# The input and weights of the per-layer projection move from the expert ring's extra slots to other tiles

## The chip, the cores and the metric

The kernel runs on one core of a Trainium2 chip. The metric is the device time in microseconds (us) of one execution; the time of a kernel is the median of its runs. All data are float32.

## What is computed

A two-layer decoder step for 256 prompt tokens and 8 decode tokens (264 columns, `T`), width 1024 (`D`). Layer 0 mixes with a Mamba-2 block, layer 1 with native sparse attention. Each layer ends in the same tail, which is where the change lies:

```python
def moe(h, router_w, router_bias, w_gate, w_up, w_down):
    score = sigmoid(h @ router_w)                  # 16 experts in 4 groups
    # the best group by score + bias, the two best experts in it, gates normed to 1
    out = 0
    for e in range(16):
        hid = silu(h @ w_gate[e]) * (h @ w_up[e])  # 1024 -> 512
        out = out + gate[..., e:e + 1] * (hid @ w_down[e])
    return out

def layer_tail(x, mix, p_i, ...):
    h = layer_norm(ALPHA * x + mix)
    h = layer_norm(ALPHA * h + moe(h, ...))
    return h + sigmoid(h @ ple_gate) * (p_i @ ple_proj)
```

`p_i @ ple_proj` is the per-layer projection: 256 to 1024, eight output tiles of 128 by 264.

## The kernel before

**Layout and staging.** Activations are kept with features on the 128 partitions and tokens along the free axis: `xT`, `acc` and `ple` are tiles of [128, 8, 264]. The program has four blocks one after the other: the Mamba block, `tail(0)`, the attention block, `tail(1)`. In each block every engine has an instruction stream of its own, and semaphores order them. All waits are written by hand.

**Expert weights.** An expert's gate, up and down matrices are each one unit of 2 MiB, [128, 4096]. Experts are taken in pairs, so a pair has six units: `n = 6 i + r`, where r = 0, 1 is gate, 2, 3 is up and 4, 5 is down. Units 48 and 49 are the two halves of `ple_gate`. Unit n lies in slot `n % 8`. Slots 0 to 5 are in `expert_ring`, which lives through the whole program; slots 6 and 7 are the tile `expert_ring_more` (`ring2`), which exists only in the tail. Slots 0 to 5 are loaded ahead of the tail or at its start (in the second tail units 3 to 5 are issued in the tail itself). All unit loads are issued by SP, in order of n. From unit 8 on SP waits until the slot is free: units 8 and 9 and 10 and 11 wait for the gate and the up half of pair 0 (`gu_done`), units 12 and 13 for its down half (`down_done`), and so on for later pairs (L979 to L985 of the program).

**The projection.** Its input `pT` (264 KB) and its weights `wple` (1 MB) lie in slot 6, that is in `ring2[:, 0]`. So SP's unit loads 6 and 7 stand behind a wait for the last projection: `sp.wait_ge(e_proj, KD * (L + 1))`. TensorE runs `project(0)` and `project(1)` before the router's rank matmuls and `project(2)` to `project(7)` after the first slot matmul (L1031). Tile m goes to one of two PSUM banks, and ScalarE copies it to `ple[:, m, :]` (L1197); `project(m)` waits for the copy of tile m - 2. `ple` is read only at the end of the tail (L1381).

**The start of pair 0.** ScalarE writes the token rows to HBM (L1194), POOL gathers the rows of a pair's 128 slots back (L1252) once these writes have landed and the slot numbers are there, TensorE transposes them (`turn_rows`, L1082), ScalarE packs them into `xg` (`pack`, L1204), and `gate_up(0)` begins (L1097). `pack(0)` stands behind all eight copies of `ple` in ScalarE's stream. After `gate_up(0)` come `other_slots` (L1057), `turn(0)` (L1106) and `down(0)` (L1119), then `gate_up(1)`. For pairs 1 and on, `scatter(i - 1)` (L1130) stands between `gate_up(i)` and `turn(i)`.

Of the kernel before, what the change touches and what calls it, by code (L numbers as in the profile page):

```python
# [20 lines left out]
P = 128  # L21
D = 1024
KD = D // P
SEQ = 256
DB = 8
T = SEQ + DB
# [13 lines left out]
NE, FF, EG = 16, 512, 4  # L40
# [18 lines left out]
def trunk(nc, I, O):  # L59
    root = ExitStack()  # L60
    with root:
# [842 lines left out]
        def tail(L, out=None):  # L904

            ld_p, e_done, e_sig, e_out, e_proj, e_pre = ple_sems
# [5 lines left out]
            with ExitStack() as st:  # L912
# [3 lines left out]
                ple = sb("ple_projected", [P, KD, T])  # L916
                acc = sb("acc", [P, KD, T])
                ring2 = sb("expert_ring_more", [P, 2, CH])
# [5 lines left out]
                xg = sb("x_packed", [P, KD, 2 * CAP])  # L924
                sg = sb("silu_gate", [P, FF])
                hid = sb("hid", [P, FF])
                ht = sb("hid_T", [P, NF, 2 * CAP])
# [5 lines left out]
                sel1 = sb("slot_onehot", [P, 3, NE * CAP])  # L933
                idxf, idxi, gcol = sb("slot_token", [P, NP2]), sb("slot_token_int", [P, NP2], I32), sb("slot_gate", [P, NP2])

                pT = ring2[:, 0, 0:2 * T].rearrange("p (k t) -> p k t", k=2)
                wple = ring2[:, 0, 2 * T:2 * T + 2 * D].rearrange("p (k n) -> p k n", k=2)
                scT = sg[0:NE, 0:T]
                xtok = [xrow[:, 0, :], xrow[:, 1, :], ys[:]]
                over = xrow[:].rearrange("p a b -> p (a b)")  # L940
# [5 lines left out]
                ob = [st.enter_context(nc.psum_tensor(f"mo{L}{n}", [P, 512], F32)) for n in range(4)]  # L946
# [19 lines left out]
                with nc.Block() as block:  # L966
                    @block.sync
                    def _(sp):
                        sp.dma_start(pT, I["pT"][L].rearrange("(k p) t -> p k t", p=P)).then_inc(ld_p, 16)
                        sp.dma_start(wple, I["ple_proj"][L].rearrange("p (k n) -> p k n", k=2)).then_inc(ld_p, 16)  # L970
                        if L == 1:
                            for n in range(3, 6):
                                load_unit(sp, L, n, unit(n))
                        sp.wait_ge(e_proj, KD * (L + 1))
                        for n in range(6, 8):
                            load_unit(sp, L, n, unit(n))
                        for n in range(8, 6 * NP2 + 2):
                            i, r = (n - 8) // 6, (n - 8) % 6
                            if r < 4:  # L979
                                sp.wait_ge(gu_done, n2 + 2 * i + 1 + r // 2)  # L980
                            else:
                                sp.wait_ge(down_done, n1 + i + 1)
                            load_unit(sp, L, n, unit(n))

                        def over_load(e):  # L985
                            sp.wait_ge(o_dve, NDV * e + 1)
                            for w, name in enumerate(("moe_w_gate", "moe_w_up", "moe_w_down")):
                                src = I[name][bass.ds(NE * L + e, 1)].rearrange("a p n -> (a p) n")
                                sp.dma_start(ring[:, 1, w * CH:(w + 1) * CH], src).then_inc(o_ld, 16)
                        sp.wait_ge(r_over, L + 1)  # L990
                        sp.wait_ge(gu_done, n2 + 2 * NP2)
                        sp.wait_ge(down_done, n1 + NP2)
                        overflow(sp, over_load)
                        if L == 0:
                            page = [page_number(sp, n) for n in range(2 * NPG)]
                            load_cmp(sp, 0, page)
                            sp.wait_ge(ln_sems[0], 2 * L + 2)
                            for c in range(2):
                                load_chunk(sp, c, I["nsa_w_in"][c])
                            sp.wait_ge(e_done, 4)  # L1000
                            load_cmp(sp, 1, page)
                        if out is not None:
                            for m in range(0, KD, 2):
                                sp.wait_ge(e_out, KD * L + m + 2)
                                store(sp, out[:, m:m + 2, :], xT[:, m:m + 2, :])

                    @block.tensor
                    def _(pe):
                        tr, mm = nc.tensor.transpose, nc.tensor.matmul
                        ln_a.pe(pe)  # L1010

                        for k in range(KD):
                            ln_a.out_ready(pe, k)
                            last = mm(hb[0][0:NE, 0:T], rw[:, k, :], xT[:, k, :], start=k == 0, stop=k == KD - 1)  # L1014
# [9 lines left out]

                        def project(m):
                            if m == 0:
                                pe.wait_ge(ld_p, 32 * L + 32)
                            if m >= 2:
                                pe.wait_ge(e_pre, KD * L + m - 1)
                            for k in range(2):  # L1030
                                last = mm(ob[2 + m % 2][:, 0:T], wple[:, k, m * P:(m + 1) * P], pT[:, k, :], start=k == 0, stop=k == 1)  # L1031
                            last.then_inc(e_proj, 1)

                        turn_x(0)
# [2 lines left out]
                        for q, (t0, n) in enumerate(tile3):  # L1037
                            last = tr(hb[1][0:n, q * NE:(q + 1) * NE], scT[:, t0:t0 + n], ident[0:NE, 0:NE])
# [144 lines left out]
                    def _(act):  # L1183
# [9 lines left out]
                                act.wait_ge(r_xtok, 6 * L + c + 1)  # L1193
                                act.dma_start(x_rows[L][t0:t0 + n, :], xtok[c // 2][0:n, :]).then_inc(r_rows, 16)  # L1194
                        for m in range(KD):
                            act.wait_ge(e_proj, KD * L + m + 1)
                            A_(ple[:, m, :], ob[2 + m % 2][:, 0:T], ACT.Copy).then_inc(e_pre, 1)  # L1197

                        def pack(i):
# [960 lines left out]
```

## Time and profile before

| | us |
|---|---|
| median of 3 runs | 1167.97 |
| lowest and highest run | 1164.39, 1169.42 |
| the profiled execution, device time | 1171.1 |
| its span, first to last instruction | 1169.3 |
| TensorE busy | 1051.3 (90%) |
| VectorE busy | 469.3 (40%) |
| ScalarE busy | 297.0 (25%) |
| DMA over the span | 347.36 MB, mean 297 GB/s |

The first tail lies at about 300 to 600 us of the span, the second at 843 to 1169. PE is TensorE's matmuls, PEld its weight loads (beside them), DVE is VectorE, ACT ScalarE, POOL GpSimd; SPq, ACTq and POOLq are the instructions with which these engines issue DMAs. PEclk is the share of TensorE's full clock that was granted: 1.0 is 2.4 GHz, 0.5 is 1.2 GHz, and a mean between them is a stretch that had some of both. Brackets behind an instruction give the idle time of its engine ahead of it and what ended it. Matmuls are pipelined, so a busy PE isn't PE at its peak.

### The profile page before, as it was taken

The page shows a single profiled execution, that of the slowest core. Times are in us where ns is not written, and L with a number is a line of the kernel's source. Part 1 is how long each engine was busy: PE and PEld are TensorE (multiplying, and loading weights), DVE is VectorE, ACT ScalarE, POOL GpSimd, SP SyncE. Part 2 cuts the span into 40 slices and gives each one's busy share as a digit, 9 for nine tenths or more (in the row PEclk, how much of TensorE's full clock was granted, in tenths as well). Part 3 has the DMA queues.
Part 4 walks back from the last instruction along what each step waited for, and adds up shares of the span by engine and source line. Part 5 has one row for each costly group of instructions (what it writes and reads, how often), then busy time and mean ns, then how long its engine had stood idle before and what let it go on. Part 6 is the DMA issues. An engine that isn't in the chain of part 4 may idle for free. (4 is left out here: it accounts for less than half of the span.)

```text
span 1169.3 us, 14744 instructions
## 1 busy us (share of the span) xinstructions
PE 1051.3 (90%) x5243; PEld 658.4 (56%) x5243; DVE 469.3 (40%) x1383; ACT 297.0 (25%) x765; POOL 133.3 (11%) x121
## 2 busy tenths in 40 slices
PE   7899998698799999899799989779989999989868
PEld 5688775587554444344477875345755344444347
DVE  2769898932331112011355977472161111111132
ACT  2211798700321111111220015362051011101031
POOL 0000013300001000000004724452000000000000
PEclk9899998799988999999999998889988999999989
DMA  8744696675959999999556975949368899999901
GB/s 287 248 163 149 220 278 215 198 281 198 399 225 408 427 429 428 425 427 428 213 216 235 339 262 178 370 136 382 128 265 370 363 427 426 428 428 426 417 4 38
DMA packets 88943, 347.36 MB, mean 297 GB/s; under 512 B 14690, under 2 KB 52578, under 8 KB 72322
## 3 DMA queue, kind: packets, MB, share of 16 engines
q1 hardware_dynamic: 81186, 313.57, 69.3%
q10 hardware_dynamic: 5376, 24.40, 5.3%
q0 software_dynamic: 2304, 8.39, 1.8%
q8 instruction: 45, 0.74, 0.3%
q14 instruction: 32, 0.26, 0.1%
HBM read 331.66 MB, written 23.04 MB: 303 GB/s over the span
## 5 line engine op out<-in xcount | busy, mean ns | idle before, releaser
L1097 PE MATMUL mh<-expert_ring,x_packed 128*64 128x512 f32 x768 | 173.0, 606 | 14.6 <-DMA expert_ring<-in_moe_w_up 12.7
L1349 DVE TENSOR_TENSOR hid<-mh,silu_gate 128x512 f32<-128x512 f32 x16 | 11.1, 692 | 374.8 <-PE mh L1097 325.9
L1097 PEld LDWEIGHTS mh<-expert_ring,x_packed 128*64 128x64 f32 x768 | 58.2, 140 | 126.3 <-issue 124.3
L1119 PE MATMUL mo<-expert_ring,hid_T 128*64 128x512 f32 x384 | 89.1, 618 | 1.4 <-ACT hid_T L1218 1.4
L495 PE MATMUL ss<-xT,expert_ring 128*128 128x264 f32 x384 | 90.0, 395 | 0.0
L1563 PE MATMUL na<-xT,expert_ring 128*128 128x264 f32 (+1 forms) x336 | 78.8, 398 | 6.1 <-DMA expert_ring<-in_nsa_w_in 3.3
L495 PEld LDWEIGHTS ss<-xT,expert_ring 128*128 128x128 f32 x384 | 73.8, 195 | 13.8 <-issue 0.8
L1563 PEld LDWEIGHTS na<-xT,expert_ring 128*128 128x128 f32 (+1 forms) x336 | 64.6, 193 | 20.2 <-DMA expert_ring<-in_nsa_w_in 4.1
L506 PE MATMUL ss<-xT,expert_ring 128*128 128x264 f32 x256 | 64.1, 406 | 6.1 <-ACT z L385 6.1
L1179 PE MATMUL mg<-acc,expert_ring 128*128 128x264 f32 x256 | 61.7, 406 | 7.2 <-ACT acc L883 7.2
L1097 PE MATMUL mh<-expert_ring_more,x_packed 128*64 128x512 f32 x256 | 58.3, 609 | 7.7 <-DMA expert_ring_more<-in_moe_w_up 3.6
L1252 POOL DMA_INDIRECT x_rows_packed<-x_rows,slot_token_int x16 | 15.6, 973 | 430.6 <-DVE slot_token_int L1312 219.2
L609 PE MATMUL ss<-conv_out,expert_ring 128*128 128x264 f32 x256 | 59.2, 394 | 4.9 <-DVE conv_out L838 4.2
L1179 PEld LDWEIGHTS mg<-acc,expert_ring 128*128 128x128 f32 x256 | 51.4, 202 | 17.5 <-issue 8.0
L506 PEld LDWEIGHTS ss<-xT,expert_ring 128*128 128x128 f32 x256 | 49.3, 198 | 19.5 <-ACT z L385 9.3
L1119 PEld LDWEIGHTS mo<-expert_ring,hid_T 128*64 128x64 f32 x384 | 27.4, 142 | 55.0 <-issue 51.2
L609 PEld LDWEIGHTS ss<-conv_out,expert_ring 128*128 128x128 f32 x256 | 49.7, 195 | 14.2 <-DVE conv_out L838 4.6
L1218 ACT ACTIVATE hid_T<-mo 128x512 f32<-128x512 f32 x16 | 9.6, 599 | 171.8 <-PE mo L1106 171.8
L1097 PEld LDWEIGHTS mh<-expert_ring_more,x_packed 128*64 128x64 f32 x256 | 20.1, 140 | 44.3 <-issue 41.9
L1227 ACT ACTIVATE y_slots<-mo 128x512 f32<-128x512 f32 x32 | 17.4, 595 | 108.8 <-PE mo L1119 108.8
L1130 PE MATMUL mo<-scatter_gates,y_slots 128*128 128x264 f32 x128 | 40.6, 399 | 2.4 <-ACT y_slots L1227 2.4
L126 POOL TENSOR_TENSOR expert_ring<-expert_ring,pos_softmax 128x1024 f32<-128x1024 f32 x14 | 39.4, 2839 | 20.6 <-DMA expert_ring<-in_cmp_pages 20.6
(377 smaller groups left out, 1541.1 us busy)
## 6 DMA issues: line engine op xcount, KB each, us to landing
expert_ring<-in_moe_w_down SPq DMA_DIRECT2D x24, 2048.0 KB, 22.3
expert_ring<-in_moe_w_gate SPq DMA_DIRECT2D x24, 2048.0 KB, 17.2
expert_ring<-in_moe_w_up SPq DMA_DIRECT2D x24, 2048.0 KB, 23.5
expert_ring<-in_ssd_w_in SPq DMA_DIRECT2D x10, 2048.0 KB, 7.9
expert_ring_more<-in_moe_w_gate SPq DMA_DIRECT2D x8, 2048.0 KB, 14.7
expert_ring_more<-in_moe_w_up SPq DMA_DIRECT2D x8, 2048.0 KB, 19.2
expert_ring_more<-in_moe_w_down SPq DMA_DIRECT2D x8, 2048.0 KB, 22.5
expert_ring<-in_cmp_pages SPq DMA_DIRECT2D x40, 256.0 KB, 4.5
```

Source lines behind the costliest of these rows:

```text
L126: return eng.tensor_tensor(x, x, wb[:, a:a + 1, :].unsqueeze(1).to_broadcast([P, NPG, 2, BLK]), ALU.mult)
L495: last = mm(pt[m % 4][:, 0:T], wc[:, k, ((m - 1) % 4) * P:((m - 1) % 4 + 1) * P], xT[:, k, :], start=k == 0, stop=k == KD - 1)
L506: last = mm(z_bank[:, 0:T], wc[:, k, (j % 4) * P:(j % 4 + 1) * P], xT[:, k, :], start=k == 0, stop=k == KD - 1)
L609: last = mm(o_bank[m][:, 0:T], w_at[k // 2][:, (k % 2) * D + m * P:(k % 2) * D + (m + 1) * P], cv[:, k, :], start=k == 0, stop=k == JX - 1)
L1097: last = mm(hb[w][s * CAP:(s + 1) * CAP, :], xg[:, k, s * CAP:(s + 1) * CAP], unit(6 * i + 2 * w + s)[:, k * FF:(k + 1) * FF], start=k == ...
L1119: last = mm(ob[2 + a][s * CAP:(s + 1) * CAP, :], ht[:, k, s * CAP:(s + 1) * CAP], unit(6 * i + 4 + s)[:, o:o + 512], start=k == 0, stop=k ...
L1130: mm(sc_bank[d % 4][:, 0:T], ys[:, d * P:(d + 1) * P], sgt[:, i, :], start=True, stop=True).then_inc(sc_done, 1)
L1179: last = mm(gb[m % 2][:, 0:T], wc[:, k, (m % 4) * P:(m % 4 + 1) * P], acc[:, k, :], start=k == 0, stop=k == KD - 1)
L1227: A_(ys[:, a * 512:(a + 1) * 512], ob[2 + a][:], ACT.Copy).then_inc(ys_ok, 1)
L1252: nc.gpsimd.indirect_dma_start(xrow[:, i % 2, :], None, x_rows[L][:, :], bass.IndirectOffsetOnAxis(idxi[:, i:i + 1], 0)).then_inc(row[i % ...
L1349: V.tensor_tensor(hid[:], hb[1][:], sg[:], ALU.mult).then_inc(hid_ok, 1)
L1563: last = mm(pb[m % 8][0:M, 0:T], wc[:, k, (m % 4) * P:(m % 4) * P + M], xT[:, k, :], start=k == 0, stop=k == KD - 1)
```

## The change

`pT` moves to the last two tiles of `ple` itself. The weights are split in three: the second half (k = 1) goes to `xg`, and the first half (k = 0) to `hid` and to `ht`. All three are tiles that pair 0 of the mixture writes for the first time after the projections. They are loaded by three DMAs in the place of one, so the load count that `project(0)` waits for goes from 32 to 64 per layer. SP no longer waits for `e_proj` ahead of units 6 and 7. ScalarE's copy of tile 6 writes where `pT` lies, and so waits for all eight projections; the copies of the other tiles wait as before.

```diff
--- before.py
+++ after.py
@@ -933,8 +933,9 @@
                 sel1 = sb("slot_onehot", [P, 3, NE * CAP])
                 idxf, idxi, gcol = sb("slot_token", [P, NP2]), sb("slot_token_int", [P, NP2], I32), sb("slot_gate", [P, NP2])
 
-                pT = ring2[:, 0, 0:2 * T].rearrange("p (k t) -> p k t", k=2)
-                wple = ring2[:, 0, 2 * T:2 * T + 2 * D].rearrange("p (k n) -> p k n", k=2)
+                pT = ple[:, 6:8, :]
+                wple1 = xg[:].rearrange("p k c -> p (k c)")
+                wple = lambda k, m: wple1[:, m * P:(m + 1) * P] if k else (hid, ht[:].rearrange("p f c -> p (f c)"))[m // 4][:, (m % 4) * P:(m % 4 + 1) * P]
                 scT = sg[0:NE, 0:T]
                 xtok = [xrow[:, 0, :], xrow[:, 1, :], ys[:]]
                 over = xrow[:].rearrange("p a b -> p (a b)")
@@ -967,11 +968,12 @@
                     @block.sync
                     def _(sp):
                         sp.dma_start(pT, I["pT"][L].rearrange("(k p) t -> p k t", p=P)).then_inc(ld_p, 16)
-                        sp.dma_start(wple, I["ple_proj"][L].rearrange("p (k n) -> p k n", k=2)).then_inc(ld_p, 16)
+                        sp.dma_start(wple1, I["ple_proj"][L][:, D:2 * D]).then_inc(ld_p, 16)
+                        sp.dma_start(hid[:], I["ple_proj"][L][:, 0:FF]).then_inc(ld_p, 16)
+                        sp.dma_start(ht[:].rearrange("p f c -> p (f c)"), I["ple_proj"][L][:, FF:D]).then_inc(ld_p, 16)
                         if L == 1:
                             for n in range(3, 6):
                                 load_unit(sp, L, n, unit(n))
-                        sp.wait_ge(e_proj, KD * (L + 1))
                         for n in range(6, 8):
                             load_unit(sp, L, n, unit(n))
                         for n in range(8, 6 * NP2 + 2):
@@ -1024,11 +1026,11 @@
 
                         def project(m):
                             if m == 0:
-                                pe.wait_ge(ld_p, 32 * L + 32)
+                                pe.wait_ge(ld_p, 64 * L + 64)
                             if m >= 2:
                                 pe.wait_ge(e_pre, KD * L + m - 1)
                             for k in range(2):
-                                last = mm(ob[2 + m % 2][:, 0:T], wple[:, k, m * P:(m + 1) * P], pT[:, k, :], start=k == 0, stop=k == 1)
+                                last = mm(ob[2 + m % 2][:, 0:T], wple(k, m), pT[:, k, :], start=k == 0, stop=k == 1)
                             last.then_inc(e_proj, 1)
 
                         turn_x(0)
@@ -1193,7 +1195,7 @@
                                 act.wait_ge(r_xtok, 6 * L + c + 1)
                                 act.dma_start(x_rows[L][t0:t0 + n, :], xtok[c // 2][0:n, :]).then_inc(r_rows, 16)
                         for m in range(KD):
-                            act.wait_ge(e_proj, KD * L + m + 1)
+                            act.wait_ge(e_proj, KD * L + min(m + 1 + m // 6, KD))
                             A_(ple[:, m, :], ob[2 + m % 2][:, 0:T], ACT.Copy).then_inc(e_pre, 1)
 
                         def pack(i):
```

## Rows read from the trace of the kernel before

**Rows 1.** The page's busy share of the DMA engines in tenths, 40 equal slices of 29.2 us.

```profile
DMA  8744696675959999999556975949368899999901
```

**Rows 2.** Chain that ended last, second tail: start us, us, what, count.

```profile
969.68 13.73 PE mh L1097 x64
...
995.50 6.89 PE mh L1097 x32
...
1062.00 30.46 DMA expert_ring<-in_moe_w_up
...
1092.60 8.45 PE mh L1097 x32
```

**Rows 3.** Timeline of SP: start us, us to issue, line, tiles, count.

```profile
300.89 0.47 SPq L970 DMA_DIRECT2D expert_ring_more<-in_ple_proj  x1
...
337.12 0.80 SPq L110 DMA_DIRECT2D expert_ring_more<-in_moe_w_gate  x2
...
345.83 0.80 SPq L110 DMA_DIRECT2D expert_ring<-in_moe_w_up  x2
...
370.32 1.00 SPq L110 DMA_DIRECT2D expert_ring<-in_moe_w_gate  x2
...
879.53 0.81 SPq L110 DMA_DIRECT2D expert_ring_more<-in_moe_w_gate  x2
...
915.70 0.81 SPq L110 DMA_DIRECT2D expert_ring<-in_moe_w_gate  x2
```

**Rows 4.** Stretches: us, busy us (count) by engine, PEclk, DMA share, GB/s.

```profile
324.00:325.00 1.00, 0.69 (x6) 0.70 (x6) 0.83 (x6) 0.29 (x2) 0.00 (x0) 1.00 0.25 33
...
370.00:371.00 1.00, 0.75 (x6) 0.48 (x5) 0.00 (x0) 0.68 (x2) 0.00 (x0) 1.00 0.77 311
...
914.00:915.00 1.00, 1.00 (x6) 0.28 (x4) 0.00 (x0) 0.00 (x0) 0.00 (x0) 1.00 0.04 16
...
325.00:330.00 5.00, 3.95 (x23) 3.46 (x23) 2.45 (x16) 0.00 (x0) 0.59 (x1) 0.74 0.00 0
...
338.00:370.00 32.00, 30.61 (x145) 14.02 (x145) 3.87 (x13) 3.51 (x6) 2.00 (x2) 0.89 1.00 415
...
881.00:914.00 33.00, 32.21 (x139) 16.11 (x141) 3.87 (x13) 2.92 (x5) 1.99 (x2) 0.79 0.96 405
```

**Rows 5.** Timeline of the first tail, TensorE and ScalarE: start us, us, engine, line.

```profile
321.57 1.95 PE L1031 MATMUL mo<-expert_ring_more 128*128 128x264 f32 x8
...
323.62 0.67 ACT L1197 ACTIVATE ple_projected<-mo 128x264 f32<-128x264 f32 x2 [0.38 <-PE mo L1031]
...
324.31 0.39 PE L1050 MATMUL mh<-insel,m 128*128 128x16 f32 x2 [0.79 <-DVE insel L1291]
...
328.86 8.23 PE L1031 MATMUL mo<-expert_ring_more 128*128 128x264 f32 x24
...
337.13 0.39 ACT L1197 ACTIVATE ple_projected<-mo 128x264 f32<-128x264 f32 x1 [0.50 <-PE mo L1031]
...
337.56 1.08 ACT L1204 ACTIVATE x_packed<-mg 128x512 f32<-128x512 f32 x2
...
338.70 13.95 PE L1097 MATMUL mh<-expert_ring,x_packed 128*64 128x512 f32 x64 [0.74 <-ACT x_packed L1204]
...
547.21 7.09 PE L1097 MATMUL mh<-expert_ring,x_packed 128*64 128x512 f32 x32 [1.62 <-DMA expert_ring<-in_moe_w_up]
```

**Rows 6.** DMAs issued about 300.9, 329.4 and 360.9: engine, count, KB, us to landing.

```profile
expert_ring_more<-in_ple_proj SPq DMA_DIRECT2D x1, 1024.0 KB, 20.2
...
x_rows_packed<-x_rows,slot_token_int POOLq DMA_INDIRECT x1, 4.5
...
x_rows_packed<-x_rows,slot_token_int POOLq DMA_INDIRECT x1, 11.7
```

**Rows 7.** Timeline: second write of token rows, and the first gather.

```profile
321.80 0.33 ACTq L1194 DMA_DIRECT2D x_rows<-x_rows_packed  x1
...
329.41 1.12 POOL L1252 DMA_INDIRECT x_rows_packed<-x_rows,slot_token_int  x1 [90.10 <-DVE slot_token_int L1312]
```

## The prediction, made before the changed kernel was run

> **What bounds the kernel now.** Read the DMA line of the page first [rows 1]: there are two long plateaus of nines, slices 13 to 19 and 33 to 38. These are the two mixtures of experts (one per tail), each of which streams 48 expert units and two gate units of 2 MiB. The chain of waits then says who holds the end [rows 2]. In the second mixture it runs on TensorE through pairs 0 to 3, and later it passes through transfers of moe_w_up that land 30 us after issue. From there the order is set by bytes, not by matmuls. So a tail has two halves. A front half is paced by TensorE (router, projection, pair 0). A back half is paced by the DMA engines, and the question is which instant starts the back half's clock.
>
> The timeline of SP [rows 3] answers. Units 6 and 7, which the change moves, go out at 337.12 and 879.53, when the last of the eight projections has ended. Units 8 to 11 follow when gate_up(0) frees slots. The next pair, 12 and 13, can't go before down(0) has read slots 4 and 5: 370.32 and 915.70. That is an instant of TensorE's front half. The DMA engines are idle ahead of 337.12 (no bytes at all from 325 to 330) [rows 4], which is the hole the change fills. But they are also just running empty when 12 and 13 are issued. At 370 to 371 the share is 0.77, and in the second tail they are at 16 GB/s from 914 to 915 [rows 4].
>
> The two tails are a natural experiment on whether a head start there is kept. In the first, units 8 to 11 were barely finished at 370.32; in the second there was a hole of some 2 us before 915.70. From the issue of 12 and 13 to the start of the up half of pair 7, the last one that waits for a load, the first tail takes 547.21 - 370.32 = 176.89 us [rows 3, 5] and the second 1092.60 - 915.70 = 176.90 us [rows 2, 3]. A hole ahead of that issue costs nothing. The back half starts when down(0) ends, and what was loaded before doesn't enter.
>
> **The change part by part.**
>
> *Units 6 and 7 go out behind the projection's loads* (about 302 and 845) and not at 337.12 and 879.53. They land some 12 us later, in the hole. Their first reader is gate_up(1), which starts behind down(0) and turn_rows(1). In either tail it doesn't wait for units 6 and 7 now, since they were issued 33 and 36 us earlier. Gain there: 0. Units 8 to 11 keep their issue times (gate_up(0) sets them); they find an empty queue and land earlier. Their readers are the down half of pair 0, which reads 4 and 5 and not these, and pair 1, which doesn't wait either. Gain: 0. Units 12 and 13 keep their issue time; in the second tail the queue was empty already, so 0. In the first tail an old remainder was still in the queue: at most the 1 us of the row at 370 [rows 4], and by the equal 176.9 us nothing. I take 0, with -1 to 0 as bounds. The hole isn't removed, it is moved to just before 370.
>
> *The copies of ple.* The input p now lies in columns 6 and 7 of ple, so ScalarE may write tile 6 only after all eight projections and not after the seventh. Tile 7 is unchanged in its wait but now stands behind tile 6. Today the copy of tile 7 starts at 337.13, pack(0) at 337.56, and gate_up(0) at 338.70, with nothing between them [rows 5]. After: tile 6 starts at 337.13, tile 7 behind it. Two copies back to back take 0.67 us where one takes 0.39 [rows 5], so the second costs 0.28; with a whole copy as the other bound, 0.28 to 0.39 us, straight on the path gather, pack, gate_up(0), down(0), issue of 12. In the second tail the same order holds. Sum: +0.6 to +0.8, I take +0.7. The projections themselves are not slowed: project(7) needs copies 0 to 5 only.
>
> *Two loads more per tail.* ple_proj comes in three pieces and not in one; the bytes are the same. SP spends 0.47 us on the one issue now [rows 3], so two more put everything behind them about 0.9 us later. In the first tail the projection's weights land at 300.89 + 20.2 = 321.1 [rows 3, 6] behind five units, and project(0) starts at 321.57 [rows 5]. Because the queue is full at that time, the landing follows the bytes and not the issue: 0. If it moved by the whole 0.9, project(0) would start 0.4 late, and TensorE has 0.79 us of waiting for VectorE right behind project(1) [rows 5] that takes it up. Cost 0; without that cover at most 0.4. In the second tail the loads find a short queue 20 us ahead of their use: 0. Units 3, 4 and 5 of the second tail go out 0.9 us later, which nobody notices: they are read from 888 on.
>
> *The token rows beside units 6 and 7.* This is what the change newly exposes. ScalarE writes the token rows to HBM (512 KiB issued at 321.80, as much 1.5 us before) and POOL gathers them back at 329.41 [rows 7]. The gather takes 4.5 us alone and 11.7 us beside unit loads [rows 6], so sharing costs up to 7 us per transfer. Today both have the engines to themselves: the writes are through by 325 [rows 4]. The gather is in at 333.9 and is needed when the projections end, 328.86 + 8.23 = 337.1 [rows 5]; slack 3.2 us. After the change 4.19 MB of loads and 1.05 MB of writes share the engines from 321.1. At 415 GB/s [rows 4] they are all through after 12.6 us, at 333.7, whatever the order. In the worst case the gather goes only then and lands at 338.2, that is 1.1 us late. In the best case the writes get half, finish by about 327, and the gather waits for nothing new. The second tail has nearly the same distances. Bounds 0 to +1.5 in each tail, 0 to +3 together. I take 0, because the writes are a quarter of the load's bytes, and a share of a half would clear them in 5 us.
>
> The Trainium skill ("DMA: Bandwidth & Descriptors", section on queues, rings and completion order) says that each engine goes round-robin between the queues with work, packet by packet, and that a completion mark lands only behind all earlier writes of that engine across its queues. The first half favours the small write, and the sum with it would be my 0. The second half would hold the write's completion behind load data written before it, and with it the sum would go towards the +3. The 11.7 us against 4.5 agrees with sharing, and does not say which half decides.
>
> **The sum**, against the profiled execution's own 1171.1 us (span 1169.3 and 1.8 around it): +0.7, no gain, gives 1171.8. That execution lies 3.1 us above the median of 1168.0, so the forecast for the median is 1168.0 + 0.7 = **1168.7 us**.
>
> **A disturbance of the same size.** From the issue of 6 to that of 12, the same instructions take 370.32 - 337.12 = 33.2 us in the first tail and 36.2 us in the second [rows 3]. The granted clock is 0.89 and 0.79 in these stretches [rows 4], a matter of how long it stayed at 1.2 GHz. So each tail can be off by 3 us either way, for no reason in the program. The three times before lie between 1164.4 and 1169.4.
>
> **Rivals.**
> - *The head start is kept.* If the back half's clock were running from units 6 and 7 on, taking 4.19 MB at 415 GB/s off it would save 10.1 us in each tail: 1168.7 - 20.2 = 1148.5 us. For it: both mixtures end bound by loads [rows 2]. Against: the queue runs empty before 12 and 13, and the equal 176.9 us. Chance 0.06.
> - *Token rows late, and the clock with them* (the slower side). It acts at the gather of pair 0, and decides once that lands later than 337.1. It costs up to 3 us as above. TensorE then stands idle just ahead of gate_up(0), coming out of a stretch at 1.2 GHz. If gate_up(0) (13.95 us for 64 matmuls [rows 5]) ran its first half at that clock, it would lose 7 us a tail; half of that is the likelier size. Together 0.7 + 3 + 7 = 10.7: 1178.7 us. For it: 11.7 against 4.5 us. Against: at most 1.5 us of idle time a tail, and idle gaps as long stand in that stretch already. Chance 0.07.
> - *The late rows without the clock*: up to 1171.7 us. Chance 0.10, inside the same band.
> - *The change doesn't load earlier*, since the units wait in the full queue of the first tail anyway: they go 20 us earlier all the same once it drains at 321. If not, only the 0.7 stays: 1168.7 us. Chance 0.02.
>
> **How the numbers follow.** Forecast 0.75, late rows 0.10, no earlier load 0.02, the two far cases 0.06 and 0.07. About 0.5% (5.8 us) is what a measurement of this kernel can tell from no change. Within it lie forecast, late rows and no earlier load, 0.87, less 0.04 for both tails' clock falling on one side: 0.83. Faster 0.08 (0.06 + 0.02), slower 0.09 (0.07 + 0.02). For the range I go 3 us of clock and 1 of the first tail's remainder below 1168.7, 1164.5, and 3 of clock and half of the late rows above, 1173.2. It leaves out both far cases.
>
> **What would show it.** Right: DMA bytes from 321 to 333 where there were none, an idle hole of 3 us or more before units 12 and 13 in both tails, and again 176.9 us from their issue to pair 7's up half; pack(0) 0.3 us later after the last projection. Wrong: an issue of 12 more than 1 us nearer to or farther from the last projection at equal clock, gate_up(0) waiting for the gathered rows, or project(0) waiting for its weights by more than 0.8 us. The forecast falls if 176.9 us becomes clearly less.

## The result and the profile after

The changed kernel takes 1189.67 us where the kernel before takes 1168.70; the ratio is 1.018 with an interval of 1.014 to 1.022. That is slower by about 21 us, outside the range of 1164.5 to 1173.2. One of the changed kernel's four runs took 1608.9 us at a granted clock of 0.625 and is left out of the ratio. The profiled execution took 1189.74 us with a span of 1188.0, 18.7 us more than the span before.

The DMA line of the page (40 slices, now of 29.7 us):

```profile
DMA  9753786766938999999555975949394899999900
```

The two plateaus are as long as before to within a slice [rows 1]. What changed lies ahead of them. The timeline of SP, for both tails:

```profile
302.40 4.00 SPq L110 DMA_DIRECT2D expert_ring_more<-in_moe_w_gate  x2
...
352.10 0.80 SPq L110 DMA_DIRECT2D expert_ring<-in_moe_w_up  x2
...
379.62 0.80 SPq L110 DMA_DIRECT2D expert_ring<-in_moe_w_gate  x2
...
859.30 1.11 SPq L110 DMA_DIRECT2D expert_ring_more<-in_moe_w_gate  x2
...
935.89 0.80 SPq L110 DMA_DIRECT2D expert_ring<-in_moe_w_gate  x2
```

Units 6 and 7 do go out 35 us earlier in the first tail (302.40, 337.12 before [rows 3]). But the next pair goes out at 352.10 and not 345.83, and units 12 and 13 at 379.62 and not 370.32. The first tail's start, taken as the issue of `pT`, is the same, 300.45 and 300.46. The timeline of the first tail says why:

```profile
335.36 1.11 POOL L1254 DMA_INDIRECT x_rows_packed<-x_rows,slot_token_int  x1 [96.07 <-DMA x_rows<-y_slots]
...
337.12 0.67 ACT L1199 ACTIVATE ple_projected<-mo 128x264 f32<-128x264 f32 x2 [1.39 <-PE mo L1033]
...
340.23 1.20 PE L1084 MATMUL mg<-ident,x_rows_packed 128*128 128x128 f32 x8 [3.15 <-DMA x_rows_packed<-x_rows,slot_token_int]
...
342.12 16.81 PE L1099 MATMUL mh<-expert_ring,x_packed 128*64 128x512 f32 x64 [0.69 <-ACT x_packed L1206]
...
358.86 8.62 PE L1059 MATMUL mo<-token_and_gates,slot_onehot 128*128 128x17 f32 x42
```

POOL's first gather stands at 335.36 (329.41 before [rows 7]), and its releaser is the last of ScalarE's three writes of token rows, issued 12.1 us earlier, at 323.25. TensorE waits 3.15 us for the gathered rows behind the projections. The matmuls of gate_up(0) then take 16.81 us where they took 13.95 [rows 5]. The stretches of 1 us and more (columns as in [rows 4]) show both halves, the DMA engines ahead of the gather and the clock behind it:

```profile
332.00:333.00 1.00, 1.00 (x4) 0.76 (x3) 1.00 (x2) 0.29 (x1) 0.00 (x0) 0.50 0.45 180
...
333.00:334.00 1.00, 1.00 (x4) 0.79 (x3) 0.76 (x1) 0.10 (x1) 0.00 (x0) 0.50 0.11 45
...
338.00:341.00 3.00, 0.77 (x7) 0.77 (x8) 0.00 (x0) 0.08 (x1) 0.00 (x0) 1.00 0.33 128
...
342.00:348.00 6.00, 5.88 (x14) 1.71 (x16) 0.00 (x0) 1.35 (x2) 0.00 (x0) 0.51 0.00 0
...
349.00:360.00 11.00, 11.00 (x57) 4.07 (x53) 0.69 (x1) 0.60 (x1) 0.00 (x0) 1.00 0.64 253
```

The loads and writes end between 333 and 334. There is no traffic of units from then to 353. The granted clock is 1.00 while TensorE waits, 0.51 at 342 to 348, behind the gap, and back at 1.00 from 348. The chain of waits runs through the same place in the second tail, where the writes take 12.44 us to land:

```profile
877.53 12.44 DMA x_rows<-y_slots
...
890.74 4.83 DMA x_rows_packed<-x_rows,slot_token_int
...
895.62 1.98 PE mg L1084 x8
...
898.27 16.92 PE mh L1099 x64
```

Cutting both spans at the same marks gives the whole of the 18.7 us. "Start" is the issue of `pT`; "up half" is the start of the up half of pair 7.

| stretch | before | after | difference |
|---|---|---|---|
| first tail, start to issue of units 12, 13 | 69.86 | 79.17 | +9.3 |
| from there to the up half | 176.89 | 177.04 | +0.2 |
| up half to the start of the second tail | 295.60 | 299.15 | +3.5 |
| second tail, start to issue of 12, 13 | 72.89 | 80.08 | +7.2 |
| from there to the up half | 176.90 | 177.25 | +0.3 |
| up half to the end | 76.70 | 74.86 | -1.8 |

The two front halves carry 16.5 us. In them gate_up(0) starts 3.4 and 4.2 us later against the tail's start, 7.6 together; 0.9 of the 4.2 is the transposes and the packing ahead of it, with eight transposes in 1.98 us where they took 1.04. The other 8.9 us is the same instructions taking longer: gate_up(0) +2.9 and +3.0, the slot matmuls +2.1 and -0.3, down(0) +1.0 and +0.3 (with their gaps, 5.9 and 3.0). The start isn't a steady mark to the microsecond: the first write of token rows follows it by 19.8 us in both first tails, and by 19.9 us before and 18.8 after in the second. The middle row isn't touched by the change. It is between 292.8 and 306.1 us in the profiles of the kernels below, without an order that follows their edits, so its +3.5 is taken as scatter.

### The profile page after: what moved, and what is told of

Read it like the earlier page. It is cut to its first block and busy times, and to the rows that moved or that the text cites. A ratio compares the mean times of both kernels' runs of the same rounds, so it can differ in the third digit from the quotient of the medians.

```text
span 1188.0 us, 14748 instructions
## 1 busy us (share of the span) xinstructions
PE 1060.8 (89%) x5243; PEld 660.6 (56%) x5243; DVE 468.7 (39%) x1383; ACT 296.3 (25%) x765; POOL 133.1 (11%) x121
## 5 line engine op out<-in xcount | busy, mean ns | idle before, releaser
L1099 PE MATMUL mh<-expert_ring,x_packed 128*64 128x512 f32 x768 | 180.7, 627 | 16.5 <-DMA expert_ring<-in_moe_w_up 14.2
L1565 PE MATMUL na<-xT,expert_ring 128*128 128x264 f32 (+1 forms) x336 | 75.7, 387 | 7.1 <-DMA expert_ring<-in_nsa_w_in 4.3
L506 PE MATMUL ss<-xT,expert_ring 128*128 128x264 f32 x256 | 64.2, 406 | 6.0 <-ACT z L385 6.0
L126 POOL TENSOR_TENSOR expert_ring<-expert_ring,pos_softmax 128x1024 f32<-128x1024 f32 x14 | 39.3, 2833 | 19.9 <-DMA expert_ring<-in_cmp_pages 19.9
```

The source lines that it names most:

```text
L126: return eng.tensor_tensor(x, x, wb[:, a:a + 1, :].unsqueeze(1).to_broadcast([P, NPG, 2, BLK]), ALU.mult)
L506: last = mm(z_bank[:, 0:T], wc[:, k, (j % 4) * P:(j % 4 + 1) * P], xT[:, k, :], start=k == 0, stop=k == KD - 1)
L1099: last = mm(hb[w][s * CAP:(s + 1) * CAP, :], xg[:, k, s * CAP:(s + 1) * CAP], unit(6 * i + 2 * w + s)[:, k * FF:(k + 1) * FF], start=k == ...
L1565: last = mm(pb[m % 8][0:M, 0:T], wc[:, k, (m % 4) * P:(m % 4) * P + M], xT[:, k, :], start=k == 0, stop=k == KD - 1)
```

## The experiments

Theory A: the early loads keep the DMA engines busy, the writes of token rows land late, the gather with them, and TensorE's clock falls behind the gap. Rivals: the new tiles and the pieces of the load cost by themselves (B); the head start has a worth that something hides (C). The times below stand beside the median of the kernel before in the same measurement, 1167 to 1169 us. The ratio in brackets is an estimate of its own with its interval, and differs by up to 0.2% from the quotient of the two medians.

**Only the tiles are new.**

```diff
+                        sp.wait_ge(e_proj, KD * (L + 1))
                         for n in range(6, 8):
                             load_unit(sp, L, n, unit(n))
```

> The changed kernel with the wait for the last projection put back ahead of units 6 and 7: input and weights lie in the new tiles and come in four loads, but units 6 and 7 go out when they did before. Theory A (the early loads take the DMA engines from the token rows, so the first gather lands late, and TensorE falls to 1.2 GHz behind the gap): all of the 20 us goes, only the copy order stays, 0.3 us a tail: about 1168.5 us, within 3 us of the kernel before; the writes of token rows are through 3 us after the last is issued, the gather goes at 329.4 and lands at 333.9. Rival B (the new tiles, the pieces of ple_proj or the order of the copies cost): stays at 1185 to 1190.

Measured: 1169.06 us, ratio 1.0003 (0.9983 to 1.0023). Rival B is out. The tiles, the three pieces of `ple_proj` and the order of the copies together cost nothing that the times can show; the whole loss comes from issuing units 6 and 7 early.

**Units 6 and 7 behind the writes, and behind the gather.** The line put in is `sp.wait_ge(r_rows, 48 * (L + 1))` in the first and `sp.wait_ge(r_row0, 16 * (4 * L + 1))` in the second.

> The changed kernel, with SP waiting for the token rows' writes (not for the projections) ahead of units 6 and 7. They go out at about 326 and run beside the first gather. Theory A in its form A1 (what shares the engines with unit loads drains with them, to the end of the loads' bytes): loads through at about 338.5, gather in at 338 to 340, gate_up(0) 1 to 3 us late and the clock low behind it, 1174 to 1182 us. Form A2 (a short transfer gets about half of the engines): gather in by 335, nothing late, 1168 to 1170 us. Rival B: 1185 to 1190 us. Rival C (the head start is worth something once the rows aren't late): below 1164 us.

> The changed kernel, with SP waiting for the first gather's landing ahead of units 6 and 7: they go out at about 334, 3 us ahead of the last projection's end, and share the engines with nothing the front half needs. Theory A, with the back half counted from the end of down(0): as the kernel before, 1167 to 1170 us, and again 176.9 to 177.3 us from the issue of units 12 and 13 to pair 7's up half. Rival C (the head start is worth what it is long): 3 us a tail less, 1162 us. Rival B: 1185 to 1190 us.

Measured: 1181.42 us behind the writes (1.0122, 1.0083 to 1.0161), 1167.81 us behind the gather (1.0008, 0.9979 to 1.0037). In the first, units 6 and 7 go out at 324.64, and the gather at 327.58. Its issue and landing, and TensorE's wait:

```profile
x_rows_packed<-x_rows,slot_token_int POOLq DMA_INDIRECT x1, 11.0
...
338.60 1.97 PE L1085 MATMUL mg<-ident,x_rows_packed 128*128 128x128 f32 x8 [4.27 <-DMA x_rows_packed<-x_rows,slot_token_int]
...
341.25 16.02 PE L1100 MATMUL mh<-expert_ring,x_packed 128*64 128x512 f32 x64 [0.69 <-ACT x_packed L1207]
```

The gather takes 11.0 us where it takes 4.5 alone [rows 6], and the wait of 4.27 us has 16 us of gate_up(0) behind it. Protecting the writes is not enough; the gather needs the engines as well. With both protected the loss is gone:

```profile
332.60 0.80 SPq L110 DMA_DIRECT2D expert_ring_more<-in_moe_w_gate  x2
...
332.71 1.04 PE L1085 MATMUL mg<-ident,x_rows_packed 128*128 128x128 f32 x8
```

The time is that of the kernel before. But units 6 and 7 go out only 0.1 us ahead of the transposes behind the last projection (1.6 us in the second tail, 877.45 and 879.05). So short a head start doesn't test rival C; e11_acc_later does, below.

**The gap filled.**

```diff
+                        for j in range((7, 10)[L]):
+                            mm(hb[1][:, 0:T], ones[:], xT[:, 0, :], start=True, stop=True)
                         turn_rows(0)
```

> The changed kernel with 7 (first tail) and 10 (second tail) matmuls of 128x264 added on TensorE in the place where it waits for the first gather; their result is overwritten and not used. If the loss beyond the late gather is the clock's (theory A): gate_up(0) runs at 2.4 GHz in 14 us and not in 16.8, the gather is as late as in the changed kernel; the first tail gets back 3 to 6 us and the second 3 us, 1180 to 1184 us. If the clock is set by the small slot matmuls behind gate_up(0) and not by the gap: gate_up(0) in 14 us, but 8.6 us for the slot matmuls as before, 1184 to 1186 us. If the gap has nothing to do with the clock: 1189 us or more.

Measured: 1180.54 us (1.0124, 1.0081 to 1.0168), 9 us less than the changed kernel by the medians and 6 by the ratios, with more work in it. The two intervals overlap, so the times alone don't carry it; the trace does.

```profile
342.07 13.95 PE L1099 MATMUL mh<-expert_ring,x_packed 128*64 128x512 f32 x64 [0.74 <-ACT x_packed L1208]
...
355.96 8.84 PE L1059 MATMUL mo<-token_and_gates,slot_onehot 128*128 128x17 f32 x42
...
342.00:348.00 6.00, 5.93 (x28) 2.06 (x30) 0.00 (x0) 1.30 (x2) 0.00 (x0) 1.00 0.01 3
```

gate_up(0) starts when it did in the changed kernel (342.07, 342.12), but at a clock of 1.00 and in 13.95 us. The slot matmuls behind it are slow here as well (8.84 us in this tail, 7.00 in the second), so their clock doesn't hang on the gap. The front halves of the table are 76.04 and 75.98 us here, 3.1 and 4.1 us shorter than in the changed kernel, with gate_up(0) starting within 0.3 us of where it did there. So 7.2 of the table's 8.9 us come back, and 5.9 of them are gate_up(0) (13.95 us in both tails). Why the slot matmuls are slow stays open.

**Half of the bytes, and more of them.** In the first kernel only unit 6 is early. In the second everything is as in the changed kernel, and two copies of 2 MiB from HBM to HBM are queued behind unit 7.

> The changed kernel with only unit 6 early; unit 7 waits for the last projection as before. Half the bytes share the engines with the token rows: 2.1 MB of load and 1.05 MB of writes are through 7.6 us after the projection's weights, at about 329, and land by 330.5. If the rows land when the bytes queued beside them are through (theory A1): the gather goes at 330 to 331 and lands by 335.5, ahead of the projections' end, so no loss in either tail: 1167 to 1171 us. If rows beside any load take their 12 us (A3, a fixed delay): the gather goes at 335.4 and the loss is the whole one, 1186 to 1190 us. Rival B': 1185 to 1190 us from the number of loads.

> The changed kernel with 4.2 MB more of copies (HBM to HBM, into a buffer nobody reads) queued on SP behind units 6 and 7 in each tail, so that the queue beside the token rows stays full for some 10 us longer. Units 12 and 13 wait for them in TensorE's stream, where they are long done. If rows drain with what is queued beside them (A1): the writes land near 343 to 348, the gather goes then and lands 5 us later, gate_up(0) starts 8 us or more later than in the changed kernel, 1205 us or more. If a row write beside a full queue takes its 12 us whatever is queued (A3): the writes land at 335.4 as in the changed kernel, and only the gather is slower, 11 to 12 us where it was 4.8: gate_up(0) at 349 where it was 342.1.

Measured: 1175.36 us (1.0074, 1.0044 to 1.0105) and 1211.6 us (one run). The first gather of each, with what released it, and the wait of TensorE in the second:

```profile
330.64 2.85 POOL L1256 DMA_INDIRECT x_rows_packed<-x_rows,slot_token_int  x1 [90.92 <-DMA x_rows<-y_slots]
```

```profile
345.73 1.11 POOL L1260 DMA_INDIRECT x_rows_packed<-x_rows,slot_token_int  x1 [107.19 <-DMA x_rows<-y_slots]
...
350.61 1.97 PE L1088 MATMUL mg<-ident,x_rows_packed 128*128 128x128 f32 x8 [14.58 <-DMA x_rows_packed<-x_rows,slot_token_int]
...
342.00:343.00 1.00, 0.00 (x0) 0.00 (x0) 0.00 (x0) 0.00 (x0) 0.00 (x0) 0.50 0.24 98
...
343.00:344.00 1.00, 0.00 (x0) 0.00 (x0) 0.00 (x0) 0.00 (x0) 0.00 (x0) 0.50 0.01 0
```

The landing of the rows releases POOL at 330.6, 335.4 or 345.7, for 2.1, 4.2 or 8.4 MB queued beside them (in the last, 4.2 of loads and 4.2 of copies). Each time it is 1.6 to 2.7 us after the DMA engines go quiet (329, 333.5 and 343). So form A1 holds for the writes, and the fixed 12 us is out: that number came from the size of the queue. Unit 6 alone, though, should have cost nothing by this sum, and it costs 7 us. TensorE waits 2.47 and 2.68 us for the gather there, and gate_up(0) takes 15.57 and 16.00 us. That had another cause.

**The scaling of acc.** In the kernel with one early unit POOL's gather instruction takes 2.85 us, where it takes 1.12 [rows 7]. VectorE's timeline beside it:

```profile
328.33 3.01 DVE L1311 TENSOR_TENSOR slot_onehot<-slot,slot_numbers 128x1792 f32<-128x1792 f32 x2
...
331.26 1.24 DVE L1336 TENSOR_SCALAR acc<-xT 128x2112 f32<-128x2112 f32 x1
```

```diff
-                        dve_step(dve, V.tensor_scalar(acc[:], xT[:], ALPHA, None, ALU.mult))
@@ behind the start of pair 0 @@
+                                dve_step(dve, V.tensor_scalar(acc[:], xT[:], ALPHA, None, ALU.mult))
```

> e5_one_early with VectorE's scaling of acc (128x2112, 1.24 us) moved behind the start of pair 0. In e5_one_early the rows landed at 330.6, as the bytes said, but POOL's gather instruction then took 2.85 us and 3.44 us where it takes 1.1, and ended 1.0 us after that scaling. Theory D (the scaling keeps POOL from writing the gather's descriptors): the instruction is back at about 1.1 us, the gather lands near 335 and 883, at most 0.5 us behind the last projection, and the time falls from 1175 to 1168 to 1171 us. If POOL was slow for another reason (unit 7 or the end of unit 6 beside it): 2.8 us again, 1175 us.

The diff is against the kernel with one early unit. Measured: 1169.01 us (1.0006, 0.9975 to 1.0036), so the 7 us are gone.

```profile
330.04 1.69 POOL L1256 DMA_INDIRECT x_rows_packed<-x_rows,slot_token_int  x1 [91.22 <-DMA x_rows<-y_slots]
...
328.72 3.01 DVE L1311 TENSOR_TENSOR slot_onehot<-slot,slot_numbers 128x1792 f32<-128x1792 f32 x2
...
335.46 1.09 PE L1086 MATMUL mg<-ident,x_rows_packed 128*128 128x128 f32 x8 [0.42 <-DMA x_rows_packed<-x_rows,slot_token_int]
```

The gather instruction is at 1.69 us, not at 1.1 as expected, and it ends at 331.73, the same instant as VectorE's one-hot comparison. In the second tail it takes 2.71 us and ends at 874.53, beside a comparison that ends at 874.64. With the scaling in place it ended 1.0 and 0.9 us behind the scaling. So POOL's instruction ends with, or just behind, whichever of these two runs last. In the kernel before it started 0.24 us ahead of the comparison and wasn't held up. Theory D holds for the scaling, which was moved. That the comparison does the same is read from its timing in two tails; no run moves it. The 0.42 us that TensorE waits here have no loss of clock behind them (gate_up(0) 13.95 us).

This kernel also settles rival C. Unit 6 goes out 33 us earlier than unit 7 (301.98 and 335.08 in the first tail). If a head start were worth its length, 2.1 MB less to load, at the 415 GB/s of [rows 4], would save 5 us a tail. The time is that of the kernel before.

**The late gather without any sharing.** The first try held the gather in the kernel before until the sixth copy of `ple`:

```diff
                                 pool.wait_ge(r_rows, 48 * (L + 1))
+                                pool.wait_ge(e_pre, KD * L + 6)
```

> The kernel before, unchanged in its loads and tiles, with POOL holding the first gather of each tail until the sixth copy of ple is done, at 335.8 and 878.2 where it went at 329.4 and 871.5. No transfer shares the engines with the rows. If the late gather is all that the change costs (theory A): gate_up(0) starts about 3.5 us late in the first tail and 2.5 to 3 us in the second, the clock falls behind the gap, and the time is 1180 to 1188 us. If the sharing costs in a second way (slower unit loads, slower rows beside others later): 1174 us or less, the late start alone.

Measured: 1195.85 us (1.0247, 1.0181 to 1.0313), outside both expectations. The experiment wasn't what it was meant to be.

```profile
332.14 1.11 POOL L1253 DMA_INDIRECT x_rows_packed<-x_rows,slot_token_int  x1 [92.75 <-ACT ple_projected L1197]
...
332.65 0.80 SPq L110 DMA_DIRECT2D expert_ring_more<-in_moe_w_gate  x2
...
344.07 1.97 PE L1082 MATMUL mg<-ident,x_rows_packed 128*128 128x128 f32 x8 [11.45 <-DMA x_rows_packed<-x_rows,slot_token_int]
```

Units 6 and 7, issued 0.5 us behind the gather, shared the engines with it, and TensorE waited 11.45 us. It does show how narrow the kernel before is. The gather must have landed, or nearly so, when units 6 and 7 go out, and there it has only because these wait for the projections (333.9 and 337.12). The second try holds units 6 and 7 until the gather has landed:

> The kernel before with its first gather held back as in e6_late_gather, and units 6 and 7 held until it has landed, so that this time nothing at all shares the engines with the rows (in e6_late_gather units 6 and 7 went out 0.5 us behind the gather and made it 12 us long, which was not meant). Theory A, the late gather and the clock behind it are the whole cost: gather 5 us, in at 340, gate_up(0) 3 to 4 us late, issue of units 12 and 13 some 76 to 79 us behind the tail's start where it was 69.9 and 72.9; 1178 to 1190 us. If the changed kernel lost its time by sharing in another way: 1168 to 1174 us.

Measured: 1183.27 us (1.0132, 1.0091 to 1.0173).

```profile
332.14 1.12 POOL L1254 DMA_INDIRECT x_rows_packed<-x_rows,slot_token_int  x1 [92.72 <-ACT ple_projected L1198]
...
336.95 1.97 PE L1083 MATMUL mg<-ident,x_rows_packed 128*128 128x128 f32 x8 [4.33 <-DMA x_rows_packed<-x_rows,slot_token_int]
...
339.61 16.87 PE L1098 MATMUL mh<-expert_ring,x_packed 128*64 128x512 f32 x64 [0.69 <-ACT x_packed L1205]
```

The issue of units 12 and 13 stands 76.7 and 80.7 us behind the tails' starts (79.2 and 80.1 in the changed kernel). With nothing sharing the engines, a late gather alone makes a gap of 4.3 us in either tail, the slow gate_up(0) behind it (16.87 and 16.88 us), and 16 us of loss. That is theory A's chain without its first link.

**Can the head start be used?** In both profiles, before and after, units 12 and 13 go out at the end of down(0), and the back half takes the same time from there. So the slot matmuls of pairs 1 to 7 ahead of it were spread between the matmuls of gate_up(0), first in the kernel before:

```diff
                                 for k in range(KD):
+                                    if i == 0 and (8 * w + k) % 2 == 1 and 8 * w + k < 14:
+                                        j = 1 + (8 * w + k) // 2
+                                        slot_last.append(slot_tokens(j, ob[1], (j - 1) * (1 + NE)))
```

> The kernel before, with the 21 slot matmuls of pairs 1 to 7 set one by one between the matmuls of gate_up(0) and not in a row behind it. They took 6.6 us and 8.8 us there (first and second tail), weight loads for the most part, and TensorE fell to 1.2 GHz behind them. If the back half starts with the issue of units 12 and 13, at the end of down(0), and the weight loads hide under the 512-column matmuls: that issue comes 4 to 6 us earlier in the first tail and 6 to 10 us in the second, and the time falls by as much, 1152 to 1160 us, again with 176.9 us from there to pair 7's up half. If the DMA engines can't start earlier because units 8 to 11 still occupy them: 1163 to 1167 us. If weight loads don't hide: 1168 us.

Measured: 1177.04 us (1.0079, 1.0045 to 1.0113).

```profile
345.25 0.81 SPq L110 DMA_DIRECT2D expert_ring<-in_moe_w_up  x2
...
355.18 0.80 SPq L110 DMA_DIRECT2D expert_ring<-in_moe_w_down  x2
...
364.50 0.81 SPq L110 DMA_DIRECT2D expert_ring<-in_moe_w_gate  x2
...
547.92 7.09 PE L1102 MATMUL mh<-expert_ring,x_packed 128*64 128x512 f32 x32 [2.69 <-DMA expert_ring<-in_moe_w_up]
```

Units 12 and 13 go out 64.2 us behind the start, 5.7 us earlier than before, and the up half comes 183.4 us later and not 176.9. Start to up half is 247.6 us, where the kernel before had 246.8. Of the 5.7 us, 4.5 don't come from the spreading: units 6 and 7 already go out 32.2 us behind the start and not 36.7, as they do in e1_tiles_only and e6_late_gather too (32.1 and 32.2). The spread matmuls hold the gate half up, so units 8 to 11 go out later against gate_up(0) (11.2 and 21.2 us behind 334.0, where it was 7.1 and 14.0 behind 338.7). They still fill the DMA engines when 12 and 13 are issued (share 1.00 from 364 to 365). None of my three outcomes foresaw a loss. From the start, both tails are within 1 us of before, and 10 us of this one execution lie in the untouched middle. From the start of gate_up(0), which leaves out the scatter ahead of it, the up half comes after 213.9 and 213.3 us, where it was 208.5 and 211.5 before and 210.0 twice in e1_tiles_only. By that mark the spreading costs 7 us, most of the 9 of the median. The second form sets the slot matmuls in the up half only, and units 6 and 7 behind the gather, in the changed kernel's tiles:

> e3_after_gather (new tiles, units 6 and 7 behind the gather) with the slot matmuls of pairs 1 to 7 set between the matmuls of the up half of gate_up(0). e8_spread showed that an earlier issue of units 12 and 13 (64 us behind the start and not 70) is given back in full when units 8 to 11 still fill the DMA engines: 183.4 us from it to pair 7's up half, not 176.9. So the back half starts at the later of two instants: the end of down(0), and the DMA engines being through with units 8 to 11, which go out 8.7 us behind gate_up(0)'s start. Here that second instant is some 32 us behind gate_up(0)'s start, 0 to 3 us earlier than down(0) ended before: 1163 to 1168 us. If the head start counts fully once down(0) isn't the limit: below 1160 us. If the DMA engines' order of bytes is all and the spread matmuls only stretch gate_up(0): 1168 us or more.

Measured: 1171.99 us (1.0024, 0.9994 to 1.0053), not the 1163 to 1168 that I expected. Start to up half is 250.1 and 247.3 us; in e3_after_gather, which it varies, it is 245.8 and 247.1. So nothing is gained here either. No version beats the kernel before. Equal to it within their intervals are this one, the change with only its tiles, the one with its loads behind the gather, and the one with unit 6 early and the scaling moved.

## Why the prediction was wrong, point by point

**What bounds the kernel** held. From the issue of units 12 and 13 to pair 7's up half it is 176.8 to 177.3 us in the first and second tail of the kernel before, of the changed one and of every experiment but e8_spread and e9_spread_second_half (180.3 to 183.4 in these), with DMA engines that had not run empty at all ahead of that issue (first tail before) or had for 3.6 us (first tail after, 376 to 379.6; the hole that the prediction named as a sign). e8_spread adds the condition that I had left out: this holds only when units 8 to 11 are through by then, or nearly so. The head start was worth nothing, as forecast.

**The copies of ple, the loads in three pieces and the late landing of weights** held, as far as the times can show (1.0003 for all of them together). The copies were priced too high: in the profile of e1_tiles_only gate_up(0) starts 1.90 and 1.91 us behind the first transpose, where it was 1.77 and 1.78, so 0.13 us a tail and not 0.35. In that profile project(0) also waits 0.66 us for its weights, which it didn't in [rows 5], and the 0.79 us that TensorE waited for VectorE behind project(1) are gone in exchange, as the prediction said. In e3_after_gather that wait is 1.27 us, over the 0.8 that the prediction named as a sign, and the time is still that of the kernel before.

**Token rows beside units 6 and 7** is the step that failed first: bounds of 0 to +1.5 us in each tail, 0 taken. Measured: +3.4 and +4.2, and gate_up(0) waited for the gathered rows, which the prediction had listed as a sign of being wrong. The bytes of the worst case were right. I had put their end at 333.7, and the engines went quiet between 333 and 334. Two terms were wrong. The writes were not "through by 327" at half of the engines; they landed behind the last of what was queued beside them, and released the gather at 335.4. And I had counted the gather from the end of the bytes and not from that release, which is 1.6 us and more behind it: 335.4 + 4.8 = 340.2, where my bound was 338.2. The row of 11.7 against 4.5 us stood in the text, but I took the value at the end that it spoke against. The Trainium skill's rule ("DMA: Bandwidth & Descriptors", queues, rings and completion order), that a completion mark lands only behind all earlier writes of its engine across queues, is the half that the traces agree with: the release by the writes' landing moves with the load queued beside them, from 330.6 to 345.7. Which mechanism does it no run here isolates.

**The clock behind the gap** is the second step that failed: the sum put it at nothing, and it stood as a rival at 0.07, priced at 7 us for both tails. It is what happened, with 8.9 us in the longer instructions, 5.9 of them in gate_up(0), and 7.2 us got back by filling the gap. The price was near and the chance wasn't. I had argued that idle gaps as long stand in that stretch already. About 1 us of idle stood there at most; the gap is 3.2 and 5.0 us, and 4.3 us in the kernel with nothing but a late gather. With 0.4 us (e11_acc_later) the clock stays.

**The sum.** +0.7 was forecast; the slower rival's 1178.7 is 11 us short. Its +10.7 is 8.0 below the 18.7 of the two profiles: 4.6 for the late start (7.6 for 3), 1.9 for the clock and 3.5 for the untouched middle, less 1.3 for the small rows of the table and the 0.7 of the copies, which is inside the late start. The other 3 us are luck of the executions: the profiled one before lay 3.1 us above the median that the forecast started from, the one after lies on its own. The range had left the rival out altogether. Two slips decide nothing: 3 and 1 us below 1168.7 is 1164.7, not 1164.5, and a queue that drains at 321 lets units 6 and 7 run 16 us earlier than 337, not 20.

## What to carry to other kernels

A wait that seems to guard only a buffer can also be what keeps a large transfer away from a small one on the critical path. Before moving a bulk load earlier, list the small transfers that will then run beside it, and price each to the end of the whole queue plus the landing. A gap on TensorE can cost again in the matmuls behind it: here gaps of 2.5 to 5.0 us cost 1.6 to 3.0 us in gate_up(0), without growing steadily with the gap. And an idle stretch of the DMA engines is worth filling only if the next load that waits for a slot could go earlier too.

## What the runs showed of the hardware that was not expected

The last of 1 MB of writes to HBM landed 12.4 us after its issue with 4.2 MB of loads queued on another engine's queue, 6.8 us after with 2.1 MB, and 22.1 us after with 8.4 MB, of which half were copies within HBM (second tails of the changed kernel, e5_one_early and e7_more_behind). Alone it was through 2.5 us after (e2_after_writes, from 322.12 to the issue of unit 6 at 324.64). Gathers into SBUF aren't held that long: the sixteen of the kernel before land at most 12.3 us after issue, 11.3 at the median, beside unit loads whose medians are 15 to 24 us. Why reads back and writes out differ here is open.

POOL's indirect gather instruction was drawn out from 1.1 to 2.9 and 3.4 us by VectorE's work beside it (e5_one_early). The Trainium skill ("SBUF — State Buffer", SBUF: two separate sides) says that while VectorE runs an operation in a fast two-port mode, GpSimd cannot write the descriptors of its DMAs. The trace agrees for the scaling of [128, 2112], if that runs in such a mode, which no row shows: without it the instruction no longer lasted past the comparison. The same section of the Trainium skill says that a VectorE operation with two inputs in SBUF locks out a GpSimd operation that reads SBUF. The comparison has two such inputs and the timing agrees, but no run isolates it. That POOL's instruction ends 0.9 to 1.0 us behind the scaling and within 0.1 us of the comparison no run here explains.
